# Where the gate's low-rank inputs are made in a retention and gated-attention block on one core

## The chip, the cores and the metric

One core of a Trainium2 chip runs the whole kernel. The metric is the device time of one execution in microseconds (us); lower is better. The kernel before took 1732.63 us (median of three runs, 1731.37 to 1732.99).

## The reference

One block of a diffusion backbone for 256 latent and 256 context tokens of width 2048. Both are normalised and modulated to h and hc, projected by w_in (2048 x 11296; the context tokens only by its first 3616 columns), and go through four retention heads and four gated-linear-attention heads, whose outputs are gated, merged and projected; a SwiGLU FFN follows. What the change touches is the gate of the attention heads:

```
p  = h  @ w_in                                  # h: (256, 2048)
pc = hc @ w_in[:, :3616]                        # hc: (256, 2048)
ga, gac = p[:, 3584:3616], pc[:, 3584:3616]     # 2 x 16 low-rank gate inputs for each token
z  = a_low[..., d*16:(d+1)*16] @ gla_a_up[d] + gla_a_bias[d]      # d = 0 forward, 1 backward
la = log_sigmoid(z) / 16                        # decay of each key, for latent and context tokens
```

Modulation comes from `silu(c) @ w_mod + b_mod`, six pieces of 2048 columns. The first two pieces (shift and scale of the first sub-layer) are needed at once; the other four are used only later.

## The kernel before

**Split products.** Nearly all products are made in fp32r with both operands split into a high and a low part. A weight slot is 256 rows of a weight matrix by 512 columns (512 KB). For each slot SP (the DMA queue) loads `raw`, ACT copies it to `w_hi` (L607), DVE subtracts to `w_lo` (L990), and PE makes h_hi x w_hi, h_lo x w_hi and h_hi x w_lo (`products`, L1516, L1520, L1528). `raw` has 8 buffers, `w_hi` and `w_lo` have 4 (SPLIT), so ACT splits a slot once PE has used the one four slots before (`w_used`), and SP reloads a `raw` buffer once DVE has read it.

**Stages.** (1) The opening: the modulation's first two pieces as plain fp32 products of the padded conditioning columns, `c_pad`, in four column groups of 32 (L1572); x and ctx are normalised and turned into `xr_t` (128 x 16 x 512, fp32: columns 0 to 255 of each k are the latent tokens, 256 to 511 the context tokens), scaled there by DVE, and split into `h_hi`, `h_lo`, `hc_hi`, `hc_lo`. Products of block 0 for both kinds of tokens and of block 1 for the latent ones are already made in it. (2) Context blocks 1 to 6 of 512 columns each, from `ctx_block`: block 1 makes only the context tokens' products, in banks 6 and 7, eight slots of 2.72 us; blocks 2 to 6 make both, eight slots of 5.44 us, alternating between banks 0 to 3 (blocks 2, 4, 6) and 4 to 7. (3) Latent blocks from column 3616 on (`lat_block`), two banks each, with the gates' small steps placed between slots by `at_pre(p)`, p counting slots. (4) Heads, up projections, output projection, FFN.

**Evacuation.** After a block PE's banks are copied by ACT into `stage` (`stage_ctx`, four copies at L615) and stored by DMA (L620). ACT does this in its fixed order: for block b in the middle of its splits for block b+1, and for block 6 ahead of the first split of latent block 0. PE waits for `staged[3]` before it writes the same banks again, and before latent block 0 for the copies of block 6.

**Late modulation.** The other four pieces of w_mod are summed on DVE, beside the products: `acc` += w_mod row chunk x silu(c). A chunk is 128 x 2048 (1 MB, loaded into one of two `wm` buffers at L325), chunk number n is k = n mod 16 of piece n div 16; the first of a piece is a `tensor_scalar` (L999), the others a `scalar_tensor_tensor` (L1002). The load of chunk n+2 waits until chunk n has been used. `chunks_at(b, j, half)` says which chunks DVE takes in context block b ahead of (half 0) or behind (half 1) its split of slot j, and SP follows the same table. In the kernel before chunks 0 to 3 stand in block 1, behind slots 1, 3, 5 and 7, and 4 to 47 are spread evenly over blocks 2 to 6. `acc` lies where `xr_t` lay (both at offset 0, 32 KB).

**The gate inputs.** At the end of block 6 PE makes them from the split h: `ga_w` (128 x 16 x 32) has been split by ACT (L714) and DVE (L1093) into `ga_hl`, and 64 products with 64 weight columns (high and low parts of both directions) and 256 token columns write bank 4 (L1667, L1668). ACT and DVE copy them to `al_t[0]` and `al_t[1]` (L723, L1103), with a row of ones for the bias. PE multiplies them by `a_up` at p = 4 and p = 12 (L1682); `a_up` holds the up weights twice, for the high and the low rows, so this product also adds the parts.

**POOL** (GpSimd) loads the constants, `ga_w` and `a_up` in a fixed order once the opening's modulation is done.

Of the kernel before, what the change touches and what calls it, by code (L numbers as in the profile page):

```python
# [40 lines left out]
OPEN_CHUNKS = 4  # L41
# [27 lines left out]
def build(nc, x, c, ctx_in, c_ctx, w_mod, b_mod, norm_mix_pre, norm_mix_post, norm_ffn_pre, norm_ffn_post,  # L69
# [10 lines left out]
    with ExitStack() as ctx:  # L80
# [72 lines left out]
        ga_hl = reg("ga_hl", [P, KT, 2, 2, LOW], 82, F32R)  # L153
# [10 lines left out]
        al_t = [reg("al_t0", [P, 4 * P], 90), reg("al_t1", [P, 4 * P], 84)]  # L164
# [105 lines left out]
        def chunks_at(b, j, half):  # L270

            if b == 1:
                return [j // 2] if (j % 2, half) == (1, 1) else []
            at = 16 * (b - 2) + 2 * j + half
            return [n for n in range(OPEN_CHUNKS, 3 * KT) if (n - OPEN_CHUNKS) * 80 // (3 * KT - OPEN_CHUNKS) == at]
# [119 lines left out]
        def _(pool):  # L395
# [28 lines left out]
            pool.memset(al_t[1][:, :], 1.0).then_inc(S("gate_rows_set"), 1)
# [170 lines left out]
        def _(act):  # L595
# [117 lines left out]
            act.wait_ge(S("ga_landed"), 16)  # L713
            act.activation(ga_hl[:, :, :, 0, :], ga_w[:, :, :].rearrange("p k (d l) -> p k d l", d=2), ACT.Copy)\  # L714
                .then_inc(S("ga_split"), 1)


            def at_pre(p):
                if p == 3:
                    act.wait_ge(S("ga_done"), 1)  # L720
                    act.wait_ge(S("gate_rows_set"), 1)
                    for r in (0, 64):
                        act.activation(al_t[0][r:r + 2 * LOW, :], bank(4)[0:2 * LOW, :], ACT.Copy).then_inc(S("al_ready"), 1)  # L723
# [260 lines left out]
        def _(dve):  # L984
# [97 lines left out]
            for b in range(1, CTX_BLOCKS):  # L1082
# [9 lines left out]
            dve.wait_ge(S("ga_split"), 1)  # L1092
            dve.tensor_tensor(ga_hl[:, :, :, 1, :], ga_w[:, :, :].rearrange("p k (d l) -> p k d l", d=2),  # L1093
                              ga_hl[:, :, :, 0, :].bitcast(F32), ALU.subtract).then_inc(S("ga_split"), 1)

            unit = ones[:, 0:1].broadcast_to([P, L])

            def at_pre(p):
                if p == 2:
                    dve.wait_ge(S("ga_done"), 1)  # L1100
                    dve.wait_ge(S("gate_rows_set"), 2)
                    for r in (0, 64):
                        dve.tensor_copy(al_t[1][r:r + 2 * LOW, :], bank(4)[2 * LOW:4 * LOW, :])\  # L1103
                            .then_inc(S("al_late_ready"), 1)
                    dve.memset(cum[:, :, :, 0:1], 0.0).then_inc(S("cum_zero"), 1)
                    dve.memset(ctx_cum[:, :, 0:1], 0.0).then_inc(S("cum_zero"), 1)
# [891 lines left out]
```

## Time and profile before

| | |
|---|---|
| Runs, median | 1732.63 us |
| Profiled execution, its own time | 1731.87 us |
| Its span | 1730.2 us |
| Mean granted TensorE clock | 0.998 |
| PE busy / DVE busy / ACT busy / POOL busy | 1703.4 / 1002.6 / 737.8 / 162.3 us |
| HBM traffic | 242 GB/s over the span |
| Context block 1 / blocks 2 to 6 on PE | 145.49 to 167.25 us / 167.25 to 384.85 us |
| Gate products on PE | 384.85 to 392.11 us |

Times in the rows below are microseconds from the start of the span, except where a row says ns. Engines: PE is the tensor engine, PEld its weight loads, DVE the vector engine, ACT the scalar engine, POOL GpSimd, SP the DMA queue. A plain fp32 product shows as two records for one instruction. The end of a product is modelled, so successive ones overlap in the rows; what one costs is read from start to start.

### The profile page before, as it was taken

The page shows a single profiled execution, that of the slowest core. Times are in us where ns is not written, and L with a number is a line of the kernel's source. Part 1 is how long each engine was busy: PE and PEld are TensorE (multiplying, and loading weights), DVE is VectorE, ACT ScalarE, POOL GpSimd, SP SyncE. Part 2 cuts the span into 40 slices and gives each one's busy share as a digit, 9 for nine tenths or more (in the row PEclk, how much of TensorE's full clock was granted, in tenths as well). Part 3 has the DMA queues.
Part 4 walks back from the last instruction along what each step waited for, and adds up shares of the span by engine and source line. Part 5 has one row for each costly group of instructions (what it writes and reads, how often), then busy time and mean ns, then how long its engine had stood idle before and what let it go on. Part 6 is the DMA issues. An engine that isn't in the chain of part 4 may idle for free.

```text
span 1730.2 us, 21371 instructions
## 1 busy us (share of the span) xinstructions
PE 1703.4 (98%) x7857; PEld 1377.4 (80%) x7857; DVE 1002.6 (58%) x1114; ACT 737.8 (43%) x828; POOL 162.3 (9%) x179
## 2 busy tenths in 40 slices
PE   6999999999999999999999999999999999999998
PEld 2468888887878888888888878888888888888886
DVE  2446767648966677666664654444545444444444
ACT  3334222227555354445544564444444444443442
POOL 0011000000056245220000000000000000000000
PEclk9999999999999999999999999999999999999999
DMA  9999999968988666656777576666666666766662
GB/s 366 378 383 374 360 357 347 364 257 309 377 292 266 191 205 197 208 147 217 224 264 219 170 218 185 192 186 189 188 189 191 186 192 187 262 195 194 192 193 91
DMA packets 183706, 419.68 MB, mean 243 GB/s; under 512 B 12960, under 2 KB 13312, under 8 KB 173792
## 3 DMA queue, kind: packets, MB, share of 16 engines
q1 hardware_dynamic: 167680, 375.45, 66.3%
q0 software_dynamic: 7216, 28.07, 4.8%
q10 hardware_dynamic: 8752, 15.38, 2.4%
q8 instruction: 38, 0.62, 0.1%
q14 instruction: 20, 0.16, 0.0%
HBM read 398.35 MB, written 20.50 MB: 242 GB/s over the span
## 4 chain that ended last, share of the span: by engine, by line
PE 95%; DMA 2%; DVE 1%; issue 1%; ACT 0%; DVEq 0%; SPq 0%; POOLq 0%; POOL 0%; ACTq 0%
PE ps L1516 28%; PE ps L1520 27%; PE ps L1528 27%; PE ps L1598 2%; PE ps L1572 2%; DMA raw<-in_w_mod 2%; PE ps L1614 1%; PE ps L1793 1%; PE ps L1809 1%; PE ps L1847 1%; PE ps L1764 1%; PE ps L1903 0%; PE ps L1743 0%; PE ps L1682 0%; PE ps L1561 0%
## 5 line engine op out<-in xcount | busy, mean ns | idle before, releaser
L990 DVE TENSOR_TENSOR w_lo<-raw,w_hi 128x1024 fp32r<-128x1024 f32 x492 | 608.2, 1238 | 516.4 <-ACT w_hi L607 516.3
L607 ACT ACTIVATE w_hi<-raw 128x1024 fp32r<-128x1024 f32 x488 | 516.2, 1060 | 795.4 <-PE ps L1528 783.5
L1516 PE MATMUL ps<-w_hi,h_hi 128*128 128x512 f32 x1456 | 457.6, 394 | 1.1 <-DVE h_lo L1415 1.1
L1520 PE MATMUL ps<-w_hi,h_lo 128*128 128x512 f32 x1456 | 450.2, 389 | 0.0
L1528 PE MATMUL ps<-w_lo,h_hi 128*128 128x512 f32 x1456 | 396.6, 389 | 0.0
L1520 PEld LDWEIGHTS ps<-w_hi,h_lo 128*128 128x128 f32 x1456 | 273.3, 188 | 57.5
L1528 PEld LDWEIGHTS ps<-w_lo,h_hi 128*128 128x128 f32 x1456 | 273.3, 188 | 57.1
L1516 PEld LDWEIGHTS ps<-w_hi,h_hi 128*128 128x128 f32 x1456 | 269.7, 188 | 57.0 <-ACT w_hi L607 1.5
L1002 DVE SCALAR_TENSOR_TENSOR acc<-wm,csil,acc 128x2048 f32<-128x2048 f32 x60 | 140.9, 2349 | 61.4 <-DMA wm<-in_w_mod 61.2
L1516 PE MATMUL ps<-w_hi,hid_hi 128*128 128x512 f32 x352 | 109.8, 389 | 0.0
L1520 PE MATMUL ps<-w_hi,hid_lo 128*128 128x512 f32 x352 | 109.7, 389 | 0.0
L1528 PE MATMUL ps<-w_lo,hid_hi 128*128 128x512 f32 x352 | 94.7, 389 | 0.0
L1520 PEld LDWEIGHTS ps<-w_hi,hid_lo 128*128 128x128 f32 x352 | 66.1, 188 | 13.7
L1528 PEld LDWEIGHTS ps<-w_lo,hid_hi 128*128 128x128 f32 x352 | 66.1, 188 | 13.7
L1516 PEld LDWEIGHTS ps<-w_hi,hid_hi 128*128 128x128 f32 x352 | 66.0, 188 | 13.7
L1520 PE MATMUL ps<-w_hi,hc_lo 128*128 128x512 f32 x192 | 59.1, 389 | 0.0
L1516 PE MATMUL ps<-w_hi,hc_hi 128*128 128x512 f32 x192 | 59.1, 389 | 0.0
L1528 PE MATMUL ps<-w_lo,hc_hi 128*128 128x512 f32 x192 | 57.8, 389 | 0.0
L1572 PE MATMUL ps<-raw,c_pad 128*32 128x512 f32 x256 | 46.4, 630 | 7.7 <-DMA raw<-in_w_mod 5.8
L586 POOL DMA_DIRECT2D hs<-hsd x1 | 0.7, 718 | 491.6 <-DVE hid_n L1466 491.6
L1052 DVE TENSOR_TENSOR w_lo<-raw,w_hi 128x1024 fp32r<-128x1024 f32 x16 | 19.3, 1223 | 44.6 <-ACT w_hi L680 44.6
L1516 PEld LDWEIGHTS ps<-w_hi,hc_hi 128*128 128x128 f32 x192 | 36.0, 188 | 7.5
(293 smaller groups left out, 1376.8 us busy)
## 6 DMA issues: line engine op xcount, KB each, us to landing
raw<-in_w_in SPq DMA_DIRECT2D x184, 512.0 KB, 6.4
wm<-in_w_mod SPq DMA_DIRECT2D x64, 1024.0 KB, 6.9
raw<-in_ffn_w_gate SPq DMA_DIRECT2D x88, 512.0 KB, 4.3
raw<-in_ffn_w_up SPq DMA_DIRECT2D x88, 512.0 KB, 4.4
raw<-in_ffn_w_down SPq DMA_DIRECT2D x88, 512.0 KB, 4.5
raw<-in_w_mod SPq DMA_DIRECT2D x64, 512.0 KB, 8.3
raw<-in_w_out SPq DMA_DIRECT2D x32, 512.0 KB, 4.5
px<-stage ACTq DMA_DIRECT2D x44, 256.0 KB, 5.9
```

The lines of the kernel that those rows point to most:

```text
L607: act.activation(w_hi[:, j % SPLIT, :, :], raw[:, j % RAW, :, :], ACT.Copy).then_inc(w_high, 1)
L990: dve.tensor_tensor(w_lo[:, j % SPLIT, :, :], raw[:, j % RAW, :, :], w_hi[:, j % SPLIT, :, :].bitcast(F32), ALU.subtract).then_inc(w_low, 1)
L1002: dve.scalar_tensor_tensor(out=a, in0=wm[:, b, :], scalar=csil[:, k:k + 1], in1=a, op0=ALU.mult, op1=ALU.add).then_inc(S("wm_used"), 1)
L1052: dve.tensor_tensor(w_lo[:, o % SPLIT, :, :], raw[:, place % RAW, :, :], w_hi[:, o % SPLIT, :, :].bitcast(F32), ALU.subtract)\
L1516: pe.matmul(o, hi[:, kk, c], w_hi[:, q, e, :], start=kk == 0, stop=False)
L1520: pe.matmul(o, lo[:, kk, c], w_hi[:, q, e, :], start=False, stop=False)
L1528: last = pe.matmul(o, hi[:, kk, c], w_lo[:, q, e, :], start=False, stop=kk == last_k)
L1572: last = pe.matmul(bank(6)[g * GROUP:(g + 1) * GROUP, :], c_pad[:, k, :], raw[:, place % RAW, e, :], start=k < 4, stop=k >= KT - 4, tile_p ...
L1598: last = pe.matmul(bank(n), t[:, 2 * i + e, m * P:(m + 1) * P], w[:, q, e, :], start=i == 0 and r == 0 and a == 0, stop=i == 7 and r == 2 ...
L1614: last = pe.matmul(bank(4 + m), t[:, 2 * i + e, m * P:(m + 1) * P], w[:, q, e, :], start=i == 0 and a == 0, stop=i == 7 and a == 5)
L1764: last = pe.matmul(bank(6, 2)[:, e * L + m * P:e * L + (m + 1) * P], g_arg[:, 1, e, key * P:(key + 1) * P], g_arg[:, 0, e, qry * P:(qry + ...
L1793: last = pe.matmul(bank(4, 2)[:, a * L:(a + 1) * L], r_kt[:, 2 * (a // 2) + f, (a % 2) * P:(a % 2 + 1) * P], r_qt[:, f, :], start=f == 0, ...
```

## The change

The gate inputs are made from `xr_t`, the unsplit fp32 h and hc, by plain fp32 products in block 1, after its third slot. Products k = g mod 4 go to column group g, so four partial sums lie in partitions 32g to 32g+31 of bank 0. ACT copies group 0 to `al_t`, DVE adds groups 1, 2 and 3 in three steps ahead of its chunks and splits of slots 0, 1 and 2 of block 2, and ACT copies the sum to rows 64 to 95. PE waits for the third addition before block 2, since that writes bank 0. Because `acc` lies over `xr_t`, DVE's chunk 0 now waits for the products: only chunk 0 is left in block 1, behind its last slot, and chunks 1 to 47 are spread over blocks 2 to 6. There is one `al_t` for both directions; `a_up` has zero rows for the other direction instead of a second copy. The split of `ga_w`, the 64 products at the end of block 6 and the copies behind them go.

```
-OPEN_CHUNKS = 4
+OPEN_CHUNKS = 1
...
             if b == 1:
-                return [j // 2] if (j % 2, half) == (1, 1) else []
+                return [0] if (j, half) == (7, 1) else []
             at = 16 * (b - 2) + 2 * j + half
             return [n for n in range(OPEN_CHUNKS, 3 * KT) if (n - OPEN_CHUNKS) * 80 // (3 * KT - OPEN_CHUNKS) == at]
...
             pool.wait_ge(S("mod_cols_done"), MOD_BLOCKS)
+            pool.dma_start(ga_w[:, :, :], w_in_k[:, :, C_GA:C_GA + 2 * LOW]).then_inc(S("ga_landed"), 16)
+            pool.memset(al_t[:, :], 1.0).then_inc(S("gate_rows_set"), 1)
...
             pool.wait_ge(S("mask_ready"), 1)
-            pool.memset(al_t[0][:, :], 1.0).then_inc(S("gate_rows_set"), 1)
+            pool.memset(a_up[:, :, :], 0.0).then_inc(S("gate_rows_set"), 1)
+            pool.wait_ge(S("gate_rows_set"), 2)
             for r in (0, 64):
                 for d in range(2):
-                    for c in range(2):
-                        pool.dma_start(a_up[r + LOW * c:r + LOW * (c + 1), d, :], gla_a_up[d])\
-                            .then_inc(S("a_up_landed"), 16)
+                    pool.dma_start(a_up[r + LOW * d:r + LOW * (d + 1), d, :], gla_a_up[d]).then_inc(S("a_up_landed"), 16)
...
(ACT, in the loop over blocks b and slots j, ahead of split(S_CTX + 8 * b, j))
+                    if b == 2 and j == 0:
+                        act.wait_ge(S("ga_done"), 1)
+                        act.wait_ge(S("gate_rows_set"), 1)
+                        act.activation(al_t[0:2 * LOW, :], bank(0)[0:2 * LOW, :], ACT.Copy).then_inc(S("al_part"), 1)
+                    if b == 2 and j == 3:
+                        act.wait_ge(S("al_part"), 4)
+                        act.activation(al_t[64:64 + 2 * LOW, :], al_t[0:2 * LOW, :], ACT.Copy).then_inc(S("al_part"), 1)
...
(DVE, in the loop over blocks b)
                 for j in range(8):
+                    if b == 2 and j < 3:
+                        dve.wait_ge(S("al_part"), j + 1)
+                        dve.tensor_tensor(al_t[0:2 * LOW, :], bank(0)[GROUP * (j + 1):GROUP * (j + 2), :], al_t[0:2 * LOW, :],
+                                          ALU.add).then_inc(S("al_part"), 1)
                     for n in chunks_at(b, j, 0):
                         add_chunk(0, n, *chunk_of(n))
                     split(S_CTX + 8 * b, j)
+                    if b == 1 and j == 7:
+                        dve.wait_ge(S("ga_done"), 1)
                     for n in chunks_at(b, j, 1):
                         add_chunk(0, n, *chunk_of(n))
...
+            def gate_inputs():
+
+                pe.wait_ge(staged[3], 1)
+                pe.wait_ge(S("ga_landed"), 16)
+                for k in range(KT):
+                    g = k % 4
+                    last = pe.matmul(bank(0)[g * GROUP:(g + 1) * GROUP, :], ga_w[:, k, :], xr_t[:, k, :], start=k < 4,
+                                     stop=k >= KT - 4, tile_position=(0, g * GROUP))
+                last.then_inc(S("ga_done"), 1)
...
                         products(s, j, 2 * j, KT - 1, CTX[2:], 6)
+                        if j == 2:
+                            gate_inputs()
...
             ctx_block(S_CTX + 8, 1, 1)
+            pe.wait_ge(S("al_part"), 4)
             with pe.Fori(0, 2) as i:
...
             ctx_block(S_CTX + 48, 6, 0)
             pe.wait_ge(staged[3], 6)
-            pe.wait_ge(S("ga_split"), 2)
-            for n, (hi, lo) in enumerate(((h_hi, h_lo), (hc_hi, hc_lo))):
-                o = bank(4)[0:4 * LOW, n * L:(n + 1) * L]
-                for k in range(KT):
-                    w = ga_hl[:, k, :, :, :].rearrange("p d a l -> p (d a l)")
-                    pe.matmul(o, w, hi[:, k, :], start=k == 0, stop=False)
-                    last = pe.matmul(o, w, lo[:, k, :], start=False, stop=k == KT - 1)
-            last.then_inc(S("ga_done"), 1)
...
(PE, at_pre, p = 4)
-                        pe.wait_ge(S("al_ready"), 2)
-                        pe.wait_ge(S("al_late_ready"), 2)
-                        pe.wait_ge(S("a_up_landed"), 16 * 10)
+                        pe.wait_ge(S("al_part"), 5)
+                        pe.wait_ge(S("a_up_landed"), 16 * 6)
```

The table of chunks changes the order of DVE's work. DVE's queue of the kernel before, from the first split of block 1 (`x2` is two in a row) to the first of block 2; `acc<-wm` rows are the chunks, `w_lo` rows the splits:

```order
L990 TENSOR_TENSOR w_lo<-raw,w_hi 128x1024 [waits w_high_ready] x2
L999 TENSOR_SCALAR acc<-wm,csil 128x2048 [waits wm_landed0]
L990 TENSOR_TENSOR w_lo<-raw,w_hi 128x1024 [waits w_high_ready] x2
L1002 SCALAR_TENSOR_TENSOR acc<-wm,csil,acc 128x2048 [waits wm_used,wm_landed1]
L990 TENSOR_TENSOR w_lo<-raw,w_hi 128x1024 [waits w_high_ready] x2
L1002 SCALAR_TENSOR_TENSOR acc<-wm,csil,acc 128x2048 [waits wm_used,wm_landed0]
L990 TENSOR_TENSOR w_lo<-raw,w_hi 128x1024 [waits w_high_ready] x2
L1002 SCALAR_TENSOR_TENSOR acc<-wm,csil,acc 128x2048 [waits wm_used,wm_landed1]
L1085 CAST mask<-mask_f 128x896 [waits consts_landed]
L1002 SCALAR_TENSOR_TENSOR acc<-wm,csil,acc 128x2048 [waits wm_used,wm_landed0]
L990 TENSOR_TENSOR w_lo<-raw,w_hi 128x1024 [waits w_high_ready]
```

The same stretch of DVE's queue in the changed kernel, up to the third addition (`al_t<-ps,al_t`):

```order
L984 TENSOR_TENSOR w_lo<-raw,w_hi 128x1024 [waits w_high_ready] x8
L993 TENSOR_SCALAR acc<-wm,csil 128x2048 [waits wm_landed0,ga_done]
L1079 CAST mask<-mask_f 128x896 [waits consts_landed]
L1083 TENSOR_TENSOR al_t<-ps,al_t 32x512 [waits al_part]
L996 SCALAR_TENSOR_TENSOR acc<-wm,csil,acc 128x2048 [waits wm_used,wm_landed1]
L984 TENSOR_TENSOR w_lo<-raw,w_hi 128x1024 [waits w_high_ready]
L996 SCALAR_TENSOR_TENSOR acc<-wm,csil,acc 128x2048 [waits wm_used,wm_landed0]
L1083 TENSOR_TENSOR al_t<-ps,al_t 32x512 [waits al_part]
L984 TENSOR_TENSOR w_lo<-raw,w_hi 128x1024 [waits w_high_ready]
L996 SCALAR_TENSOR_TENSOR acc<-wm,csil,acc 128x2048 [waits wm_used,wm_landed1]
L1083 TENSOR_TENSOR al_t<-ps,al_t 32x512 [waits al_part]
```

All eight splits of block 1 now stand together, chunks 0 to 3 behind them, and the three additions between those chunks.

PE's queue in the changed kernel from the last slot of block 1 into block 2 (the branch and the ISA rows open the loop over blocks 2 to 5); the kernel before has the same rows there with no wait for `al_part`:

```order
L1507 MATMUL ps<-w_hi,hc_hi 128x512 x2
L1511 MATMUL ps<-w_hi,hc_lo 128x512 x2
L1519 MATMUL ps<-w_lo,hc_hi 128x512 [waits w_low_ready]
L1519 MATMUL ps<-w_lo,hc_hi 128x512 x3
L1661 UNCONDITIONAL_BRANCH [waits al_part]
L1661 ISA
L1502 ISA [waits stage_written3]
L1507 MATMUL ps<-w_hi,h_hi 128x512 [waits w_high_ready]
```

All of block 2 stands behind that branch.

PE's queue of the changed kernel where block 6 ends and latent block 0 begins:

```order
L1519 MATMUL ps<-w_lo,h_hi 128x512 x2
L1519 MATMUL ps<-w_lo,hc_hi 128x512 x2
L1507 MATMUL ps<-w_hi,h_hi 128x512 [waits stage_written3,w_high_ready,ones_ready]
L1507 MATMUL ps<-w_hi,h_hi 128x512
L1511 MATMUL ps<-w_hi,h_lo 128x512 x2
```

The 64 gate products that stood between the second and the third of these rows are gone; the latent block's first product stands right behind block 6.

## Rows read from the trace of the kernel before

**Rows 1.** The page, part 1: busy time, share of the span, instructions

```profile
PE 1703.4 (98%) x7857; PEld 1377.4 (80%) x7857; DVE 1002.6 (58%) x1114; ACT 737.8 (43%) x828; POOL 162.3 (9%) x179
```

**Rows 2.** Waits of PE from 145 us to the end: total, times, longest

```profile
PE ps L1793 <- ACT r_kt L822: 1.2, 1, 1.2
PE ps L1516 <- DVE h_lo L1415: 1.1, 1, 1.1
```

**Rows 3.** Timeline of PE (start, duration): first, last gate product; then latent block 0

```profile
384.85 0.28 PE L1667 MATMUL ps<-h_hi,ga_hl 128*64 128x256 f32 x1
...
392.00 0.28 PE L1668 MATMUL ps<-hc_lo,ga_hl 128*64 128x256 f32 x1
392.11 0.63 PE L1516 MATMUL ps<-w_hi,h_hi 128*128 128x512 f32 x2
392.58 0.62 PE L1520 MATMUL ps<-w_hi,h_lo 128*128 128x512 f32 x2
...
393.95 1.07 PE L1528 MATMUL ps<-w_lo,h_hi 128*128 128x512 f32 x4
```

**Rows 4.** Timeline of ACT behind block 6

```profile
385.05 1.09 ACT L615 ACTIVATE stage<-ps 128x512 f32<-128x512 f32 x2 [20.12 <-PE ps L1528]
...
386.98 1.08 ACT L607 ACTIVATE w_hi<-raw 128x1024 fp32r<-128x1024 f32 x1
```

**Rows 5.** Timeline of PE in the opening: one set of four column groups, then the next work

```profile
103.42 1.06 PE L1572 MATMUL ps<-raw,c_pad 128*32 128x512 f32 x8
104.41 0.73 PE L1598 MATMUL ps<-w_hi,h_hi 128*128 128x512 f32 x2
```

**Rows 6.** POOL's first DMA behind the opening, and the landing of ga_w's DMA

```profile
123.77 0.70 POOL L408 DMA_DIRECT2D rows<-in_b_mod  x1 [89.23 <-PE ps L1551]
...
DMA to landing us min/median/max: 5.8/5.8/5.8
```

**Rows 7.** Timeline of PE: slot 3 of block 1, its last w_lo products, block 2

```profile
153.65 0.62 PE L1516 MATMUL ps<-w_hi,hc_hi 128*128 128x512 f32 x2
...
166.35 1.07 PE L1528 MATMUL ps<-w_lo,hc_hi 128*128 128x512 f32 x4
167.25 0.62 PE L1516 MATMUL ps<-w_hi,h_hi 128*128 128x512 f32 x2
```

**Rows 8.** Timeline of ACT: the copies of block 0's banks

```profile
146.72 2.04 ACT L615 ACTIVATE stage<-ps 128x512 f32<-128x512 f32 x4
```

**Rows 9.** Timeline of DVE: last split of block 1, chunk 3, mask; a piece's first chunk

```profile
157.72 1.23 DVE L990 TENSOR_TENSOR w_lo<-raw,w_hi 128x1024 fp32r<-128x1024 f32 x1 [0.82 <-ACT w_hi L607]
158.87 2.34 DVE L1002 SCALAR_TENSOR_TENSOR acc<-wm,csil,acc 128x2048 f32<-128x2048 f32 x1
161.13 0.62 DVE L1085 CAST mask<-mask_f 128x896 uint8<-128x896 f32 x1
...
218.60 1.29 DVE L999 TENSOR_SCALAR acc<-wm,csil 128x2048 f32<-128x2048 f32 x1 [1.45 <-DMA wm<-in_w_mod]
219.80 1.22 DVE L990 TENSOR_TENSOR w_lo<-raw,w_hi 128x1024 fp32r<-128x1024 f32 x1
```

**Rows 10.** Tile al_t: DVE's copies (ns: min, median, max)

```profile
L1103 DVE COPY al_t<-ps x2: 682/684/685, 393.0 to 393.7; 32x512 f32<-32x512 f32 x2
```

**Rows 11.** Tile wm, 160 to 200 us: nine 1 MB loads, from issue

```profile
DMA to landing us min/median/max: 4.8/6.4/8.9
```

**Rows 12.** Timelines of DVE and PE: sixth slot of block 2

```profile
195.87 1.22 DVE L990 TENSOR_TENSOR w_lo<-raw,w_hi 128x1024 fp32r<-128x1024 f32 x1
...
198.08 0.61 PE L1528 MATMUL ps<-w_lo,h_hi 128*128 128x512 f32 x2
```

**Rows 13.** Stretches: us, busy PE, PEld, DVE, ACT, POOL; PE clock, DMA share, GB/s

```profile
19.60:24.68 5.08, 0.00 (x1) 0.01 (x1) 1.44 (x2) 3.78 (x3) 0.54 (x1) 1.00 1.01 419
24.68:28.05 3.37, 3.37 (x16) 3.27 (x16) 2.41 (x6) 2.72 (x5) 0.55 (x1) 0.50 0.99 402
```

**Rows 14.** Waits of PE in the opening: total, times, longest

```profile
PE ps L1572 <- DMA raw<-in_w_mod: 5.8, 8, 2.4
```

More of the change, by code:

```diff
@@ L152, in build @@
         ga_w = reg("ga_w", [P, KT, 2 * LOW], 80)
-        ga_hl = reg("ga_hl", [P, KT, 2, 2, LOW], 82, F32R)
         la = reg("la", [P, 2, GH, 2 * L], 32)
@@ L163, in build @@
         gkc = reg("gkc", [P, MT, GH * GDK], 86)
-        al_t = [reg("al_t0", [P, 4 * P], 90), reg("al_t1", [P, 4 * P], 84)]
+        al_t = reg("al_t", [P, 4 * P], 84)
         a_up = reg("a_up", [P, 2, GH * GDK], 86)
@@ L411, in _ @@
             pool.dma_start(mask_f[:, :, :], k_mask).then_inc(S("consts_landed"), 16)
-            pool.dma_start(ga_w[:, :, :], w_in_k[:, :, C_GA:C_GA + 2 * LOW]).then_inc(S("ga_landed"), 16)
             pool.dma_start(rope[:, :, :, :], k_rope).then_inc(S("tables_landed"), 16)
             pool.wait_ge(S("mask_ready"), 1)
-            pool.memset(al_t[0][:, :], 1.0).then_inc(S("gate_rows_set"), 1)
+            pool.memset(a_up[:, :, :], 0.0).then_inc(S("gate_rows_set"), 1)
+            pool.wait_ge(S("gate_rows_set"), 2)
             for r in (0, 64):
                 for d in range(2):
-                    for c in range(2):
-                        pool.dma_start(a_up[r + LOW * c:r + LOW * (c + 1), d, :], gla_a_up[d])\
-                            .then_inc(S("a_up_landed"), 16)
+                    pool.dma_start(a_up[r + LOW * d:r + LOW * (d + 1), d, :], gla_a_up[d]).then_inc(S("a_up_landed"), 16)
                 pool.dma_start(a_up[r + 2 * LOW:r + 2 * LOW + 1, :, :], gla_a_bias.rearrange("(a d) n -> a d n", a=1))\
                     .then_inc(S("a_up_landed"), 16)
-            pool.wait_ge(S("ga_done"), 1)
-            pool.memset(al_t[1][:, :], 1.0).then_inc(S("gate_rows_set"), 1)
             pool.wait_ge(S("tables_landed"), 16)
@@ L710, in _ @@
                         store_ctx(b - 1)
+                    if b == 2 and j == 0:
[5 more added lines that the diff above has]
+                        act.activation(al_t[64:64 + 2 * LOW, :], al_t[0:2 * LOW, :], ACT.Copy).then_inc(S("al_part"), 1)
                     split(S_CTX + 8 * b, j)
-            act.wait_ge(S("ga_landed"), 16)
-            act.activation(ga_hl[:, :, :, 0, :], ga_w[:, :, :].rearrange("p k (d l) -> p k d l", d=2), ACT.Copy)\
-                .then_inc(S("ga_split"), 1)
             def at_pre(p):
[L719 to L723, printed above, removed]
                 if p in (5, 6, 7, 13, 14, 15):
@@ L1089, in _ @@
                     split(S_CTX + 8 * b, j)
+                    if b == 1 and j == 7:
+                        dve.wait_ge(S("ga_done"), 1)
                     for n in chunks_at(b, j, 1):
                         add_chunk(0, n, *chunk_of(n))
-            dve.wait_ge(S("ga_split"), 1)
-            dve.tensor_tensor(ga_hl[:, :, :, 1, :], ga_w[:, :, :].rearrange("p k (d l) -> p k d l", d=2),
-                              ga_hl[:, :, :, 0, :].bitcast(F32), ALU.subtract).then_inc(S("ga_split"), 1)
             unit = ones[:, 0:1].broadcast_to([P, L])
             def at_pre(p):
[L1099 to L1106, printed above, removed]
                 if p in (8, 17):
@@ L1110, in at_pre @@
                     dve.wait_ge(S("la_step"), 3 * d + 3)
+                    if d == 0:
+                        dve.memset(cum[:, :, :, 0:1], 0.0).then_inc(S("cum_zero"), 1)
+                        dve.memset(ctx_cum[:, :, 0:1], 0.0).then_inc(S("cum_zero"), 1)
                     dve.scalar_tensor_tensor(out=t, in0=bank(4, 4), scalar=0.0, in1=t, op0=ALU.min, op1=ALU.subtract)\
@@ L1681, in at_pre @@
                         r = slice(64 * (h % 2), 64 * (h % 2) + 2 * LOW + 1)
-                        last = pe.matmul(bank(4 + h), a_up[r, d, h * GDK:(h + 1) * GDK], al_t[d][r, :], start=True, stop=True)
+                        last = pe.matmul(bank(4 + h), a_up[r, d, h * GDK:(h + 1) * GDK], al_t[r, :], start=True, stop=True)
                     last.then_inc(S("z_done"), 1)
```

## The prediction

> **What bounds the kernel now.** The page's part 1 comes first: TensorE (PE) is busy 98% of the span, DVE 58% [rows 1]. The waits of PE after 145 us show how complete that is: two idle spells of 1.2 and 1.1 us in 1585 us [rows 2]. So from context block 1 on, every microsecond of PE work taken out is gained and every one put in is paid, unless the edit opens a wait, and nothing later can absorb a stall of PE. That makes the question a local one: what PE does at the two places touched, and what it now has to wait for there. Time on DVE, ACT and the DMA queues counts only where PE waits for its result.
>
> **Place 1, the end of context block 6: products removed.** The PE timeline shows 64 split products, each 256 columns wide, the first at 384.85, the last at 392.00, and latent block 0 begins at 392.11 us [rows 3]. Removed: 7.26 us.
>
> They covered something. Latent block 0 writes banks 0 and 1, which still hold block 6, and its first weights are split by ACT only behind the four copies out of those banks. The ACT timeline: copies from 385.05, then w_hi from 386.98 for 1.08 us, to about 388.05 [rows 4]. That is 3.2 us after block 6's end at 384.85. It cost nothing beside 7.26 us of products; with them gone PE has nothing else queued there. Add 0.1 us for the release: **3.3 us of new idle time**. The low half is no further wait: w_lo is needed four hi and four lo products later (1.8 us, from the PE rows 392.11 and 393.95 in [rows 3]), and DVE's 1.2 us beside ACT's second split finishes sooner. The copies of the gate rows (2 by ACT, 2 by DVE) also leave here; they were on no wait of PE. The queue order below them is as before.
>
> **Place 2, inside block 1: products added.** 16 plain fp32 products of 512 columns in four column groups. The same form (128x32 weights, 128x512 moving) is in the opening: eight records, which are four instructions, one for each group, run from 103.42 to 104.41 us, 0.99 us [rows 5]. Four such sets: 3.96 us at most, if each pays its own start and drain. If only streaming counted, a full-width pass of 512 columns goes by at 0.227 us (0.91 us for four, [rows 3]), four passes for a set, 3.6 us in all. I take **3.8 us**, nearer to the row of the same form. Its inputs are there: ga_w is now the first DMA that POOL issues after 123.8 us (it took 5.8 us to land [rows 6]), it is needed at 153.65, after the third slot of block 1 [rows 7]; the bank copies of block 0 end near 148.8 [rows 8].
>
> **Place 3, the start of block 2: a new wait.** PE may not overwrite bank 0 before al_part is 4, that is, before DVE has made its third addition. What stands ahead of that addition on DVE decides. After w_lo of block 1's last slot the new order is: chunk 0 (tensor_scalar), mask cast, addition 1, chunk 1, split of block 2 slot 0, chunk 2, addition 2, split of slot 1, chunk 3, addition 3. Four chunks stand there, where the kernel before had made three of them earlier in block 1, between splits, where DVE had time.
>
> Call the added product time G. It moves PE, ACT and DVE alike from slot 3 of block 1 on, so it drops out of the difference. Start to start on DVE [rows 9]: a split 1.15 us (157.72 to 158.87), a full chunk 2.26 (158.87 to 161.13), chunk 0 1.20 (218.60 to 219.80), the cast 0.6. An addition of 32x512 out of PSUM I put at 0.7, from the copy of that shape (0.68 [rows 10]). So: split at 157.72+G, chunk 0 at 158.87+G, cast 160.07+G, addition 160.7+G, chunk 1 (its data long landed) 161.4+G, split 163.6+G, chunk 2 not before 164.8+G.
>
> Chunks 2 and 3 have two buffers between them: each load is issued only when the chunk two before it is used, load 2 at 160.15+G, load 3 at 163.7+G. From issue to landing such a 1 MB load took 4.8 at least, 6.4 in the median and 8.9 us at most between 160 and 200 us [rows 11]. Chunk 2 starts at max(164.8, 160.15+L)+G, chunk 3 at the later of 4.1 us after chunk 2 (chunk, addition, split) and 163.7+L+G, and the third addition ends 3.0 us after that. With L = 4.8: 169.1, ends 172.0. With 6.4: 170.7, ends 173.6. With 8.9: 173.2, ends 176.1. All plus G. PE without the wait starts block 2 at 167.25+G [rows 7]. The stall is 4.8, **6.4** or 8.9 us; even with the data there DVE's own queue makes it about 4.7. I take the median: fewer loads compete in block 1 now, but two chunks' loads and the first raw slot of block 3 are under way together.
>
> Queued behind the waiting PE instruction is all of block 2; ACT waits for the same count before the split of slot 3, needed 16 us later, which hides it. DVE and the loads gain on PE meanwhile, worth nothing, since PE did not wait for them before. Block 2 now has 10 chunks for 9; before, w_lo of its sixth slot was ready 1.0 us ahead of PE (split end 197.1, PE at 198.1 [rows 12]). After a stall of 6 us that lead is larger, not smaller.
>
> **The clock.** In the opening PE was idle 5.08 us (19.60 to 24.68 us) and the next 3.4 us of work ran at a granted clock of 0.50, that is 1.2 GHz [rows 13]. After place 3's wait of about that length I expect one such stretch, part of it falling within the idle time: between 0 and 1.7 us (half of 3.4), and I take **1.0**. For place 1, 3.3 us of idle lies between 2.4 us, after which the clock stayed at 1.00, and 5.08 [rows 13, 14]; I put nothing and keep 1.7 as its upper end.
>
> The Trainium skill, "TensorE: Matmul & The Clock Gate", section "HAM oscillation — how this bites in real kernels", describes bursts of products with waits for data of a few microseconds between them, after each of which the engine restarts at the low clock. By that rule the idle time at place 1 brings the low clock too, and the sum would be the second rival's below. The opening's drop agrees with it; no row here has a gap of 3.3 us in the midst of work.
>
> **Sum.** -7.26 (removed) +3.8 (added) +6.4 (new wait before block 2) +3.3 (uncovered copy and split) +1.0 (clock) = **+7.2 us**. Against the profiled execution, 1731.87 us: 1739.1. The median shown lies 0.76 us above that execution, so the forecast for the median is 1739.9 us. A difference of 0.2%, 3.5 us, is about what a measurement of this kernel can tell from none. Removed with nothing on PE's path: the split of ga_w on ACT and DVE (ACT then waited 20 us), one zeroing, four DMAs of POOL, which waits for other work anyway.
>
> **Rivals.**
> - *The wait is met in time, no change.* If the third addition ends before PE is through block 1, only -7.26+3.8+3.3 = -0.2 us is left: 1732.5. For it: the last split of block 1 is ready at 158.9, 7.4 us before PE wants it at 166.35 [rows 7, 9], so DVE looks far ahead there. Against: it would have to finish at 167.25+G, and its own queue, loads apart, ends 4.7 us after that. The point from which it decides is the time of chunk 3: it would have to start 4.8 us sooner than the earliest above. Chance 0.08. Were the copies at place 1 covered as well, it would be 1729.2, faster; the ACT rows speak flatly against that: 0.03.
> - *The second idle time also drops the clock.* A wait of 3.3 us at place 1, then latent block 0 starts at 1.2 GHz: at most half of 3.4 us, less what falls in the idle time, +1.2 us, 1741.1. For it: the drop after 5.08 us; against: none after 2.4. Chance 0.15.
> - *Column groups run one after another.* Then 16 products take 16 x 0.99 = 15.8 us, +12, 1752. Against: four in 0.99 us in the opening. Chance 0.03.
> - *DVE stays behind in block 2.* One more chunk, each load 6 to 9 us: if splits of block 2 come late, another 2 to 4 us, 1743. Against: the stall itself gives the lead back. Chance 0.08.
>
> **Numbers.** The forecast as summed has 0.63. Low end: wait 4.7, products 3.6, copies 3.2, no clock loss: +4.2, so 1736.8; high end: 8.9+4.0+3.4+1.7+1.7-7.26 = +12.4, 1745.0. The low end goes to 1736.0, for a shorter addition than put; that leaves out the no-change, faster and one-after-another cases and a little more, within 2 in 10. Slower by over 0.2%: the forecast, the clock and the DVE cases, with that of the groups 0.89, less 0.02 for a wait shorter than any row gives: 0.87. Within 0.2%: 0.10. Faster: 0.03.
>
> **What would show it.** PE's timeline: no 64 products before latent block 0, but a gap near 3.3 us released by ACT's w_hi or stage; 16 products after the third slot of block 1 within 4 us; a gap of 5 to 9 us before block 2, released by DVE's al_t. DVE's timeline: three w_mod chunks between the last split of block 1 and that release, two of them behind a DMA. The granted clock at 0.5 for up to 3.4 us around it. A PE that passes into block 2 without a gap would make the forecast wrong, and so would a gap whose releaser is not al_t.

## The result and the profile after

The changed kernel takes 1745.38 us (median of 6 runs, 1744.61 to 1746.33) against 1732.64 us for the kernel before: a ratio of 1.0074, 95% interval 1.0063 to 1.0085. It is 12.7 us slower. The forecast was +7.2 us, 1739.9 us, with 1745.0 as the high end; the measured time lies 0.4 us above it. The profiled execution took 1744.80 us with a span of 1743.1, 12.9 us more than the span before.

PE's waits from block 1 to the end (total, times, longest) answer to [rows 2]. Two entries stand on top of the two of before:

```profile
PE ps L1507 <- DVE al_t L1083: 7.8, 1, 7.8
PE ps L1507 <- ACT w_hi L604: 3.2, 1, 3.2
PE ps L1787 <- ACT r_kt L816: 1.3, 1, 1.3
PE ps L1507 <- DVE h_lo L1406: 1.1, 1, 1.1
```

PE's timeline through block 1 and into block 2 (start, duration), against [rows 7]:

```profile
153.23 1.07 PE L1519 MATMUL ps<-w_lo,hc_hi 128*128 128x512 f32 x4
154.22 3.64 PE L1643 MATMUL ps<-xr_t,ga_w 128*32 128x512 f32 x32
157.80 0.73 PE L1507 MATMUL ps<-w_hi,hc_hi 128*128 128x512 f32 x2
...
170.62 1.07 PE L1519 MATMUL ps<-w_lo,hc_hi 128*128 128x512 f32 x4
179.50 1.22 PE L1507 MATMUL ps<-w_hi,h_hi 128*128 128x512 f32 x2 [7.81 <-DVE al_t L1083]
180.52 1.05 PE L1507 MATMUL ps<-w_hi,hc_hi 128*128 128x512 f32 x2
181.37 1.05 PE L1511 MATMUL ps<-w_hi,h_lo 128*128 128x512 f32 x2
```

The 16 plain fp32 products (32 records) take 3.58 us. Block 1 would end at 171.52 (its last w_lo products take 0.90 us); block 2 starts at 179.50. Behind that, two products take 0.85 us from start to start where they took 0.45: full-size products at half the rate.

DVE's timeline in the same stretch, against [rows 9]:

```profile
162.00 1.23 DVE L984 TENSOR_TENSOR w_lo<-raw,w_hi 128x1024 fp32r<-128x1024 f32 x1 [5.29 <-ACT w_hi L604]
163.14 1.28 DVE L993 TENSOR_SCALAR acc<-wm,csil 128x2048 f32<-128x2048 f32 x1
164.34 0.62 DVE L1079 CAST mask<-mask_f 128x896 uint8<-128x896 f32 x1
164.99 0.68 DVE L1083 TENSOR_TENSOR al_t<-ps,al_t 32x512 f32<-32x512 f32 x1
165.60 2.33 DVE L996 SCALAR_TENSOR_TENSOR acc<-wm,csil,acc 128x2048 f32<-128x2048 f32 x1
167.86 1.21 DVE L984 TENSOR_TENSOR w_lo<-raw,w_hi 128x1024 fp32r<-128x1024 f32 x1
171.97 2.35 DVE L996 SCALAR_TENSOR_TENSOR acc<-wm,csil,acc 128x2048 f32<-128x2048 f32 x1 [2.90 <-DMA wm<-in_w_mod]
174.35 0.69 DVE L1083 TENSOR_TENSOR al_t<-ps,al_t 32x512 f32<-32x512 f32 x1
174.97 1.20 DVE L984 TENSOR_TENSOR w_lo<-raw,w_hi 128x1024 fp32r<-128x1024 f32 x1
176.10 2.33 DVE L996 SCALAR_TENSOR_TENSOR acc<-wm,csil,acc 128x2048 f32<-128x2048 f32 x1
178.47 0.69 DVE L1083 TENSOR_TENSOR al_t<-ps,al_t 32x512 f32<-32x512 f32 x1
```

This is the queue of the forecast, row by row. The first addition ends at 165.67, the third at 179.16; what lies between is three chunks, two splits, the second addition and 2.9 us of waiting for the load of chunk 2.

The end of block 6 on PE, against [rows 3]:

```profile
399.49 0.61 PE L1519 MATMUL ps<-w_lo,hc_hi 128*128 128x512 f32 x2
403.29 0.81 PE L1507 MATMUL ps<-w_hi,h_hi 128*128 128x512 f32 x2 [3.18 <-ACT w_hi L604]
403.90 1.05 PE L1511 MATMUL ps<-w_hi,h_lo 128*128 128x512 f32 x2
```

And the granted clock (columns as in [rows 13]; the last three of a row are clock, DMA share, GB/s):

```profile
173.00:174.90 1.90, 0.00 (x0) 0.00 (x0) 1.87 (x2) 0.00 (x0) 0.00 (x0) 1.00 0.87 312
174.95:185.15 10.20, 5.65 (x13) 4.48 (x14) 7.66 (x6) 3.63 (x6) 0.00 (x0) 0.50 0.88 297
185.25:187.00 1.75, 1.75 (x9) 1.44 (x8) 0.02 (x1) 0.00 (x0) 0.00 (x0) 0.99 0.88 248
402.00:403.50 1.50, 0.21 (x1) 0.24 (x2) 0.32 (x1) 1.50 (x3) 0.00 (x0) 1.00 1.03 384
403.70:407.00 3.30, 3.30 (x10) 2.53 (x9) 3.30 (x3) 2.28 (x3) 0.00 (x0) 0.50 0.63 179
407.10:409.00 1.90, 1.90 (x9) 0.98 (x10) 1.90 (x3) 1.04 (x1) 0.00 (x0) 0.99 1.11 358
```

The clock fell at both places. At the first it stood at 0.50, that is 1.2 GHz, for 10.2 us, 5.65 of them with PE at work; at the second for 3.4 us, all of them with PE at work.

So the 12.9 us of span come from five stretches, read from start to start on PE. The table has them for all kernels of this study, each from its profiled execution; "behind block 6" runs to the end of both latent block 0's first slot and the four al_t products.

| us | block 1 starts at | block 1 and the wait behind it | block 2, first slot | rest of blocks 2 to 6 | behind block 6 |
|---|---|---|---|---|---|
| before | 145.49 | 21.76 | 5.44 | 212.16 | 12.02 |
| changed | 145.97 | 25.55 + 7.98 | 8.29 | 212.16 | 9.76 |
| e1_adds_first | 145.65 | 25.55 | 5.44 | 216.86 | 11.02 |
| e2_busy_wait | 146.69 | 33.20 | 5.58 | 212.16 | 9.78 |
| e3_busy_end | 147.22 | 33.07 | 7.03 | 212.15 | 8.21 |
| e4_table_only | 145.46 | 21.76 | 5.44 | 215.68 | 12.02 |
| e5_memset_back | 146.45 | 33.04 | 7.89 | 212.16 | 9.76 |
| e6_end_cover | 146.02 | 33.29 | 7.07 | 212.15 | 4.87 |
| e8_early_and_covered | 147.04 | 25.55 | 5.44 | 212.16 | 4.86 |
| e9_one_group | 145.86 | 43.73 | 6.91 | 212.16 | 10.78 |
| e10_ga_w_back_too | 145.41 | 25.56 | 5.44 | 214.09 | 4.87 |

Changed minus before: +0.48 (block 1 starts later), +3.79 (products), +7.98 (wait), +2.85 (first slot of block 2), -2.26 (behind block 6): 12.84 us.

### The profile page after: what moved, and what is told of

Same layout as the page of the kernel before. It is cut to its first block, busy times and chain, and to the rows that moved or that the text cites. A ratio compares the mean times of both kernels' runs of the same rounds, so it can differ in the third digit from the quotient of the medians.

```text
span 1743.1 us, 21303 instructions
## 1 busy us (share of the span) xinstructions
PE 1704.6 (98%) x7825; PEld 1374.0 (79%) x7825; DVE 1003.8 (58%) x1114; ACT 736.8 (42%) x827; POOL 160.3 (9%) x175
## 4 chain that ended last, share of the span: by engine, by line
PE 94%; DMA 2%; DVE 2%; issue 1%; ACT 1%; DVEq 0%; SPq 0%; POOLq 0%; POOL 0%; ACTq 0%
PE ps L1507 27%; PE ps L1511 27%; PE ps L1519 27%; PE ps L1589 2%; PE ps L1563 2%; DMA raw<-in_w_mod 2%; PE ps L1605 1%; PE ps L1787 1%; PE ps L1803 1%; PE ps L1841 1%; PE ps L1758 1%; DMA wm<-in_w_mod 0%; PE ps L1897 0%; PE ps L1737 0%; DVE w_lo L984 0%
```

## The experiments

**e1_adds_first.** What makes the wait: the changed kernel with the three additions ahead of chunk 0.

```
-                    if b == 2 and j < 3:
-                        dve.wait_ge(S("al_part"), j + 1)
-                        dve.tensor_tensor(al_t[0:2 * LOW, :], bank(0)[GROUP * (j + 1):GROUP * (j + 2), :], ...
...
                     if b == 1 and j == 7:
                         dve.wait_ge(S("ga_done"), 1)
+                        for g in range(3):
+                            dve.wait_ge(S("al_part"), g + 1)
+                            dve.tensor_tensor(al_t[0:2 * LOW, :], bank(0)[GROUP * (g + 1):GROUP * (g + 2), :], ...
```

> The changed kernel with DVE's three additions moved ahead of its first w_mod chunk, right behind the last split of block 1. Theory A (what stands ahead of the third addition on DVE makes the wait before block 2): the third addition ends near 165.5 us, 6 us before PE is through block 1; the wait of 7.8 us and the slow stretch behind it (2.8 us) both go, 10.7 us less than the changed kernel, about 1734.6 us. Rival B (the w_mod loads, pushed out of block 1, are what PE would wait for anyhow): PE passes into block 2 but then waits for w_lo in its first slots, with DVE behind a DMA; less than half is won, 1740 us or more.

Measured: 1739.80 us, 1.0047 (1.0030 to 1.0063) of the kernel before, whose median beside it was 1732.18. DVE's timeline (start, duration, x3 for three in a row):

```profile
162.93 2.13 DVE L1088 TENSOR_TENSOR al_t<-ps,al_t 32x512 f32<-32x512 f32 x3
164.99 1.26 DVE L993 TENSOR_SCALAR acc<-wm,csil 128x2048 f32<-128x2048 f32 x1
```

The additions end at 165.1, PE enters block 2 at 171.20 without a gap, the clock stays up: theory A for the wait. But only 5.6 us of the 10.7 were won in the medians, 5.2 us in the profiled executions. PE's waits in this run:

```profile
PE ps L1519 <- DVE w_lo L984: 4.1, 2, 2.3
PE ps L1507 <- ACT w_hi L604: 3.2, 1, 3.2
```

Blocks 2 to 6 took 4.7 us more behind their first slot: PE now waits for w_lo twice, in blocks 3 and 4, after DVE had waited for chunks. Here rival B holds, in a smaller size and later than it said. And behind block 6 the clock stood at 0.50 for 6.8 us where it had been 3.4 (11.02 for 9.76 us in the table); why, no run shows. The wait before block 2 had hidden the first of these: it gave DVE 8 us of lead.

**e4_table_only.** The same from the other side: the kernel before with the new table of chunks alone.

```
-OPEN_CHUNKS = 4
+OPEN_CHUNKS = 1
...
-                return [j // 2] if (j % 2, half) == (1, 1) else []
+                return [0] if (j, half) == (7, 1) else []
```

> The kernel before with only the new table of w_mod chunks: chunk 0 behind block 1's last split, chunks 1 to 47 spread over blocks 2 to 6; gate inputs as before. Theory A (the table costs nothing by itself, only through the additions behind it): PE enters block 2 at 167.25 without a gap; w_lo of block 2's slots may come late by 0 to 3 us since DVE has three more chunks ahead of them and no stall gives it time; 1732.6 to 1735.6 us, most likely within 1 us of the kernel before. Rival B (the loads missing from block 1 starve block 2): PE waits 5 us or more in block 2, 1738 us or more.

Measured: 1735.39 us (10 runs, 1731.74 to 1742.02) beside 1732.18: 1.0015 (1.0003 to 1.0027), in the upper part of A's range. PE's waits over the whole run:

```profile
PE ps L1528 <- DVE w_lo L990: 2.1, 4, 1.0
```

No gap before block 2, four small ones later; blocks 2 to 6 take 3.5 us more. Three chunks pushed out of block 1 cost some 3 us (0.5 to 4.7 by the interval) unless something else gives DVE that time. How much varies from run to run: the ten runs spread over 10 us, the 13 of the kernel before over 3. That the w_mod loads do this is likely but not shown, since only one of the ten was profiled.

**e2_busy_wait.** Is the slowness behind the wait the clock? 60 transposes of the identity on PE while it waits.

```
+            for _ in range(60):
+                pe.transpose(bank(3)[:, 0:P], ident[:, :], ident[:, :])
             pe.wait_ge(S("al_part"), 4)
```

> The changed kernel with 60 transposes of the identity into bank 3 (free there) between block 1 and PE's wait for al_part, 0.12 us each, some 7.1 us: the wait itself stays, only PE is busy through most of it. Theory A (the slow products behind the wait are TensorE's clock, which fell because PE was idle): the granted clock stays at 1.00 through block 2, the first slot of block 2 takes 5.44 us instead of 8.3, 2.8 us less, about 1742.6 us. Rival B (the slowness is the restart behind a branch and a wait, not the clock): first slot as slow as before, no gain, 1745.4 us.

Measured: 1743.64 us, 1.0071 (1.0054 to 1.0088). PE's timeline:

```profile
172.24 6.71 PE L1661 MATMUL ps<-ident 128*128 128x128 f32 x60
179.89 0.72 PE L1507 MATMUL ps<-w_hi,h_hi 128*128 128x512 f32 x2 [0.94 <-DVE al_t L1083]
```

Block 2 starts as late as before, but its first slot takes 5.58 us instead of 8.29, and the granted clock is 1.00 throughout:

```profile
171.50:187.80 16.30, 15.37 (x99) 13.56 (x99) 12.26 (x8) 4.70 (x7) 0.00 (x0) 1.00 0.91 319
```

Theory A. Of the 2.7 us won there, 1.7 show in the median; in the profiled execution block 1 started 0.7 us later than in the changed kernel's.

**e3_busy_end.** The same behind block 6, with 26 transposes into bank 7 ahead of latent block 0.

> The changed kernel with 26 transposes of the identity into bank 7 (free there) ahead of latent block 0, 3.1 us, beside ACT's copies and first split. Theory A (the idle time of 3.2 us there lowered the clock for 3.4 us): no stretch at 0.50 behind block 6, latent block 0 starts at the same time and its first slots run at full rate, 1.7 us less, about 1743.7 us. Rival B (the clock falls there for another reason, or the transposes end later than w_hi): no gain, 1745.4 us or more.

Measured: 1742.50 us, 1.0061 (1.0045 to 1.0078). PE's timeline:

```profile
399.48 3.00 PE L1667 MATMUL ps<-ident 128*128 128x128 f32 x26
402.83 0.69 PE L1507 MATMUL ps<-w_hi,h_hi 128*128 128x512 f32 x2 [0.35 <-ACT w_hi L604]
```

Latent block 0 starts 3.36 us behind block 6, as in the changed kernel, and at the full rate; the stretch is 8.21 instead of 9.76 us, and the clock stays up through it:

```profile
399.20:410.00 10.80, 10.45 (x58) 7.72 (x58) 7.28 (x6) 8.79 (x10) 0.00 (x0) 1.00 0.70 229
```

Theory A, 1.55 us for 1.7. The median gained 1.2 us more than expected. In the profiled execution the wait before block 2 was shorter too (7.4 us) and so was the slot behind it (7.03), and block 1 started 1.25 us later than in the changed kernel's; this edit touches none of the three.

**e5_memset_back.** The 0.48 us ahead of block 1: one run, with POOL's memset of al_t moved behind its DMAs.

```
-            pool.memset(al_t[:, :], 1.0).then_inc(S("gate_rows_set"), 1)
             for r0, n, v in ((0, 64, b_mod[2 * D:6 * D]), ...
...
             pool.dma_start(rope[:, :, :, :], k_rope).then_inc(S("tables_landed"), 16)
+            pool.wait_ge(staged[3], 1)
+            pool.memset(al_t[:, :], 1.0).then_inc(S("gate_rows_set"), 1)
```

> The changed kernel with POOL's memset of al_t moved back behind its DMAs and the first bank copies (past 149 us). Theory A (the memset at 125.0 us, beside DVE's eight scalings of xr_t, slows them): the eight scalings take 2.67 us again instead of 3.27, PE's wait for w_lo behind them 1.0 instead of 1.6 us, and everything later stands 0.5 us earlier. Rival B (the earlier DMA of ga_w or chance does it): 3.27 and 1.6 us again.

DVE's eight scalings of xr_t as one row of the timeline, in the kernel before, the changed one and this one:

```profile
124.48 2.67 DVE L383 TENSOR_SCALAR xr_t<-xr_t,scale,mod_t 128x256 f32<-128x256 f32 x8
```

```profile
124.36 3.27 DVE L382 TENSOR_SCALAR xr_t<-xr_t,scale,mod_t 128x256 f32<-128x256 f32 x8
```

```profile
125.12 2.98 DVE L382 TENSOR_SCALAR xr_t<-xr_t,scale,mod_t 128x256 f32<-128x256 f32 x8
```

Half of it: 2.98, and PE's wait for w_lo 1.3 us for 1.6 (before: 1.0). The memset costs 0.3 us; something else the other 0.3. The one time, 1744.63 us, says nothing at this size. The changed kernel's rows say which scalings are slow, and beside what:

```profile
L382 DVE TENSOR_SCALAR xr_t<-xr_t,scale,mod_t x8: 395/400/726, 124.4 to 127.2; 128x256 f32<-128x256 f32 x8
123.66 1.34 POOL L406 DMA_DIRECT2D ga_w<-in_w_in  x1 [89.12 <-PE ps L1542]
124.99 0.56 POOL L407 MEMSET al_t<- 128x512 f32 x1
```

Six of the eight take some 0.40 us each. The first, at 124.36, takes 0.73 us and ends at 125.09, just behind POOL's issue of ga_w's DMA (it ends at 125.00). The second, at 125.01, takes 0.69 and ends just behind the memset. In this run, without the memset there, only the first is slow (0.72), and in the kernel before none is (0.41 at the most).

**e6_end_cover.** Can the end be covered instead of waited out? ACT's first three splits for latent block 0 stand ahead of the copies, the al_t products ahead of the latent block.

```
-                    if j == 0 and t == 0:
+                    if j == 3 and t == 0:
                         stage_ctx(6, 0)
...
-                    pe.wait_ge(staged[3], CTX_BLOCKS)
+                    pe.wait_ge(staged[2 * t + 1], CTX_BLOCKS)
...
+                if t == 0:
+                    at_pre(4)
                 lat_block(S_LAT + 8 * t, 0, t, ...
```

> The changed kernel with place 1 covered: ACT makes its first three splits for latent block 0 before the four copies of block 6's banks, PE makes the four al_t products (p = 4) before latent block 0 instead of behind its first slot, and latent block 0 waits for the first two copies only, block 1 for all four. Theory A (copies and first split, then the clock, are the whole cost there): no gap and no low clock at the end of block 6, 3.3 and 1.7 us less, about 1740.4 us. Rival B (PE then waits for the second pair of copies, or for la): a gap reappears in the latent blocks 0 or 1, 1742 us or more.

Measured: 1738.88 us, 1.0038 (1.0023 to 1.0054). PE's timeline:

```profile
398.08 0.61 PE L1519 MATMUL ps<-w_lo,hc_hi 128*128 128x512 f32 x2
398.63 1.99 PE L1676 MATMUL ps<-al_t,a_up 33*128 33x512 f32 x8
400.55 0.73 PE L1507 MATMUL ps<-w_hi,h_hi 128*128 128x512 f32 x2
```

No gap: 4.87 us behind block 6 for 9.76. Theory A, 4.9 us for the 5.0 expected. The median is 1.5 us lower still. In the profiled execution the low clock before block 2 was shorter (6.8 us for 10.2, first slot 7.07), which would be 1.2 us of it; that the other executions had the same is not shown.

**e9_one_group.** Are four groups worth it? All 16 products in group 0, the additions left as they are, so the sums for groups 1 to 3 are left out and stale data are added instead.

```
-                    last = pe.matmul(bank(0)[g * GROUP:(g + 1) * GROUP, :], ga_w[:, k, :], xr_t[:, k, :], start=k < 4,
-                                     stop=k >= KT - 4, tile_position=(0, g * GROUP))
+                    last = pe.matmul(bank(0)[0:GROUP, :], ga_w[:, k, :], xr_t[:, k, :], start=k == 0,
+                                     stop=k == KT - 1, tile_position=(0, 0))
```

> The changed kernel with all 16 plain fp32 products in column group 0 (the additions of groups 1 to 3 then add what block 0 left in the bank, so this changes the result; the instructions are the same). Theory A (the four groups stream side by side): 16 products take 16 x 0.86 = 13.7 us instead of 3.67, everything behind them, the wait before block 2 included, moves by 10 us: about 1755 us. Rival B (plain fp32 products of 32 columns are that fast by themselves): 4 to 7 us, below 1749 us.

One run: 1754.68 us, and

```profile
154.11 13.92 PE L1643 MATMUL ps<-xr_t,ga_w 128*32 128x512 f32 x32
167.96 0.73 PE L1507 MATMUL ps<-w_hi,hc_hi 128*128 128x512 f32 x2
```

13.85 us for 3.58. Theory A: the groups run side by side. One group would have been slower than the 7.26 us of split products that were removed.

**e8_early_and_covered.** All of it put right. The products go behind slot 0 of block 1, once the first bank copy is done, and chunks 0 to 3 stay in block 1 with the old table behind it.

```
-                return [0] if (j, half) == (7, 1) else []
+                return [(3, 4, 6, 7).index(j)] if j in (3, 4, 6, 7) and half == 1 else []
...
-                pe.wait_ge(staged[3], 1)
+                pe.wait_ge(staged[0], 1)
...
-                        if j == 2:
+                        if j == 0:
                             gate_inputs()
```

with DVE's wait for the products behind its split of slot 3, the additions of e1 behind block 1's last split, ACT's copy of group 0 ahead of the split of slot 6, the memset of e5 and the end of e6.

> All of it put right: products behind slot 0 of block 1 (bank 0 is free by then), so that chunks 0 to 3 stay in block 1, behind slots 3, 4, 6 and 7, with the old table for blocks 2 to 6; the three additions together behind block 1's last split; the memset back; the end covered as in e6. Theory A (the shortened arithmetic is worth 7.26 - 3.8 = 3.5 us once no wait is opened): no wait of PE at either place, 1728.7 us, 3.5 us below the kernel before. Rival B (block 2's w_lo come late, as with the table alone): 1 to 3 us of that are lost again, 1730 to 1732 us.

Measured: 1730.02 us (11 runs, 1728.80 to 1730.84) beside 1732.04: 0.9985 (0.9976 to 0.9994), below both kernels. By the number this is rival B's range, not the 1728.7 of theory A. PE's waits from block 1 to the end are the two of before:

```profile
PE ps L1789 <- ACT r_kt L817: 1.7, 1, 1.7
PE ps L1509 <- DVE h_lo L1408: 1.1, 1, 1.1
```

From the start of block 1 to behind block 6 it takes 248.01 us where the kernel before takes 251.38: 3.4 us, as the arithmetic says (7.26 - 3.79). The median shows 2.0. Rival B's late w_lo is not seen. In the profiled execution the difference lies ahead of block 1, which starts 1.55 us later than in the kernel before, and most of that is the clock in the opening, after the idle time that [rows 13] shows there:

```profile
23.30:33.45 10.15, 7.86 (x29) 4.63 (x30) 5.54 (x9) 6.58 (x8) 1.09 (x2) 0.50 1.03 397
34.84 1.06 PE L1565 MATMUL ps<-raw,c_pad 128*32 128x512 f32 x8
```

Here it stood at 0.50 for 10.2 us, in the kernel before for 3.4. The products of the second row start at 33.50 in the kernel before, 1.3 us sooner, and the opening's last ones of this form are still 1.2 us late (121.12 for 119.91). The scalings, 2.98 us here, add the rest.

**e10_ga_w_back_too.** As e8, with the DMA of ga_w back behind the small constants.

```
-            pool.dma_start(ga_w[:, :, :], w_in_k[:, :, C_GA:C_GA + 2 * LOW]).then_inc(S("ga_landed"), 16)
             for r0, n, v in ((0, 64, b_mod[2 * D:6 * D]), ...
...
+            pool.dma_start(ga_w[:, :, :], w_in_k[:, :, C_GA:C_GA + 2 * LOW]).then_inc(S("ga_landed"), 16)
             pool.dma_start(rope[:, :, :, :], k_rope).then_inc(S("tables_landed"), 16)
```

> As e8, with POOL's DMA of ga_w also back in its old place, behind the small constants (it is needed at 150 us). Theory A (what POOL does beside DVE's eight scalings of xr_t sets their time, 2.67 us in the kernel before, 3.27 in the changed one, 2.98 with the memset back: the large DMA's issue of 1.34 us is the other half): 2.67 us again and a wait of 1.0 us for w_lo, 0.3 us less than e8, about 1729.7 us, no wait of PE at the three places. Rival B (the rest was chance): 2.98 us again.

Measured: 1729.92 us (11 runs) beside 1732.55: 0.9986 (0.9977 to 0.9995). DVE's scalings:

```profile
124.35 2.68 DVE L382 TENSOR_SCALAR xr_t<-xr_t,scale,mod_t 128x256 f32<-128x256 f32 x8
```

2.68 us and a wait of 1.0 us: theory A, the DMA's place is the other half. The 0.3 us cannot be seen in the medians of e8 and e10. In this run PE waited 1.6 us for one w_lo in block 2, behind a chunk for whose load DVE had waited 3.1 us. The kernel before had kept 1.0 us clear there [rows 12], and e8, with the same table, shows no such wait; whether the three chunks that stand later in block 1 make it likelier or it is chance in the loads stays open.

## Why the prediction was wrong

The places on PE and the chain behind the wait were right; the clock term was too small by 3.5 us, by far the largest error, and it carried the time past the range. Two smaller ones point the same way: the wait, 1.6 us, and the opening, 0.5 us. By the steps of the forecast:

- *Removed, -7.26 us.* Right: nothing of it is left on PE.
- *Products, +3.8.* Measured 3.79 on block 1, and the form's row in the opening [rows 5] was the right one to scale from. The rival of groups one after another is refuted by e9, whose 13.85 us are what it would have cost (put there at 15.8).
- *Wait before block 2, +6.4.* Measured 7.98. The chain was right to 0.2 us a row; the load's latency was mis-sized. Load 2 went out at 164.45 and chunk 2 started at 171.97, 7.5 us later, and with L = 7.5 the forecast's own formula gives 7.5. The median of nine loads up to 200 us [rows 11] was the wrong sample: the three loads issued between 150 and 162 us, in the very stretch, took 7.6 to 8.9 us. That fewer loads would compete was no help. The last 0.3 to 0.5 us lie between the third addition's end (179.16) and PE's start (179.50), and in the additions' own queueing. e1 shows the cause of the wait by taking it away.
- *Copies and first split, +3.3.* Measured 3.34; e6 takes it away.
- *Clock, +1.0 with nothing at place 1.* Measured 2.85 + 1.67 = 4.52 us. **This is the step that failed**, at both places. The forecast took the opening's one stretch of 3.4 us [rows 13] as the size of any, let part of it fall within the idle time, and capped the cost at 1.7 for each place. Behind the wait of 8 us the clock stood at 0.50 for 10.2 us, 5.8 of them behind PE's restart, and the first slot lost half of that, 2.85 us; behind the 3.3 us at place 1 it fell too. e2 and e3 show that both are the idle time's doing: the same waits with PE kept busy lose 0.1 us each. The rival that the second idle time drops the clock had 0.15 and came true, at 1.67 us for 1.2.

  The Trainium skill ("TensorE: Matmul & The Clock Gate", section "HAM oscillation — how this bites in real kernels") was right where the forecast gave it a chance of 0.15: waits of some microseconds between bursts restart PE at the low clock, here at both places.
- *Costed at nothing: the opening.* +0.48 us. The forecast looked at POOL's steps as covered, and asked only when ga_w lands; what they do to DVE beside them was not asked. e5 and e10 split it into the memset and the DMA's issue, 0.3 us each.
- *Costed at nothing: block 2 with one chunk more.* Right as the forecast said it, "the stall itself gives the lead back", and e1 and e4 show the price without the stall: 4.7 and 3.5 us over blocks 2 to 6. So the parts don't add up: the wait costs 7.98 + 2.85 us but hides some 4 of the table's. The rival's place was off; it shows in blocks 3 to 6 rather than in block 2.
- *"Met in time, no change" and "faster".* Refuted as argued: the queue of DVE was as read.

What stays open: how long the clock stays down. The five profiled kernels with the same wait, of 7.3 to 7.8 us, differ in it:

| kernel | at 0.50 for | of it behind PE's restart | first slot of block 2, over 5.44 |
|---|---|---|---|
| changed | 10.2 us | 5.8 us | 2.85 us |
| e5 | 10.2 us | 5.0 us | 2.45 us |
| e6 | 6.8 us | 3.1 us | 1.63 us |
| e3 | 6.8 us | 3.2 us | 1.59 us |
| e9 | 6.8 us | 2.8 us | 1.47 us |

The cost is about half of the third column each time; what decides the second, no run shows. Behind block 6 it was 3.4 us in three kernels (changed, e2, e5) and 6.8 in two (e1, e9). The opening does the same, and that accounts for most of the spread in block 1's start: the three kernels with 10.2 us at 0.50 there (e2, e3, e8) start block 1 at 146.69 to 147.22, the eight with 3.4 or 6.8 us at 145.41 to 146.45. The forecast had one such row and could not see this spread.

## What to carry to other kernels

Before work is moved from one place to another, ask of each place what else it covered: here 7.26 us of products hid a copy and a split of 3.3 us, and reordering two queues (e6) kept the gain without them. A wait that is placed on a bound engine costs what stands ahead of its release in the releasing engine's queue, so the release goes first (e1), and a table that spreads side work has to be moved with it (e8). An idle spell on PE like those here, of 3.3 and some 8 us, is to be priced with the low clock behind it, between 1.5 and 2.9 us, at every place where it occurs; one row at the low clock is not its size.

## What the runs showed of the hardware

Work on POOL slows DVE's tensor_scalar beside it. Eight of them, 128x256 fp32 from SBUF to SBUF, took 2.68 us beside small DMA issues, 2.98 beside the issue of one large DMA (256 KB, 1.34 us on POOL), and 3.27 with a 0.56 us memset as well (e10, e5, the changed kernel). The whole loss is in the one scaling that runs beside each: 0.73 and 0.69 us for 0.40. The Trainium skill ("SBUF — State Buffer", section "SBUF: two separate sides") says that DVE, in a mode that uses two ports, and GpSimd share a pair of ports, held by whichever starts first for its whole instruction. That the second scaling ends only behind the memset agrees with that; no row tells the mode of these scalings, and no run here separates the ports from another cause.

The low clock has no fixed length. After 8 us of idle it went down some 3.5 us into the wait and came back 5.8 us after work had begun again (174.95 to 185.15 us in the rows above lie within it), with PE at work for all of that time. In the opening, after the same 5.1 us of idle, the stretch at 0.50 was 3.4 us in the kernel before and 10.2 us in e8.
